# Router stage of a three-part transformer kernel: normed rows from TensorE transposes and ScalarE copies instead of GpSimd, slot table from bf16 products

## What is computed

```
x = layer_norm(ALPHA * x + h, ln_g[0], ln_b[0])          # 512 x 1024
g_logits = xf @ w_rg + b_rg                              # 512 x 4
g_idx = argmax(g_logits)
e_logits = (xf @ w_re + b_re).reshape(T, 4, 8)           # 512 x 32
top_v, top_i = top_k(e_logits of the group g_idx, 2)
order = argsort(flat_e)                                  # tokens' slots, sorted by expert
xbuf[slot_dest] = repeat(xf, 2)                          # rows gathered by expert
...                                                      # experts' three matmuls on xbuf
x = layer_norm(ALPHA * x + f, ln_g[1], ln_b[1])
```

## Time and profile before

| | us |
|---|---|
| median of 3 runs | 2987.75 |
| lowest, highest | 2985.99, 2991.82 |
| time of the profiled execution | 2988.24 |
| its span, first to last instruction | 2986.4 |
| PE busy in the span | 2835.5 (95%) |
| DVE, ACT, POOL busy | 2187.5 (73%), 1498.5 (50%), 497.3 (17%) |
| mean granted clock of TensorE, as a share of the full one | 0.975 |
| the router, from the mixer's last product (227.1) to the experts' first (284.3) | 57.2 |

### The profile page before, as it was taken

The page is one execution under the profiler, slowest core; times in us unless marked ns, Lnnn a source line. Parts: engine busy times, 40 slices in busy tenths (PEclk is TensorE's granted clock), DMA queues, the critical chain, the costliest instruction groups (busy, mean ns, idle before and its releaser), DMA issues.

```text
span 2986.4 us, 41805 instructions
## 1 busy us (share of the span) xinstructions
PE 2835.5 (95%) x16000; PEld 2449.8 (82%) x16000; DVE 2187.5 (73%) x2917; ACT 1498.5 (50%) x1995; POOL 497.3 (17%) x504
## 2 busy tenths in 40 slices
PE   8995999999958999999999999899999999999997
PEld 6674788888847999888888999799998888889996
DVE  6637899999978777666458776887776665687775
ACT  6823788888845444433335444454443332354443
POOL 3214011111012111110113111121111111121111
PEclk9997999999978999999999999999999999999998
DMA  5152999999945555232335646365543332355551
GB/s 215 50 174 90 349 376 373 374 374 380 375 167 140 158 162 157 94 108 88 98 99 135 180 132 177 105 163 148 171 137 99 100 99 94 99 148 156 160 159 57
DMA packets 170155, 516.25 MB, mean 173 GB/s; under 512 B 21600, under 2 KB 22112, under 8 KB 169696
## 3 DMA queue, kind: packets, MB, share of 16 engines
q1 hardware_dynamic: 130176, 422.38, 39.9%
q0 software_dynamic: 37568, 79.72, 12.6%
q10 hardware_dynamic: 2208, 11.43, 1.0%
HBM read 509.24 MB, written 12.58 MB: 175 GB/s over the span
## 4 chain that ended last, share of the span: by engine, by line
PE 81%; DVE 7%; issue 4%; ACT 3%; DMA 2%; POOL 2%; SPq 0%; DVEq 0%; ACTq 0%; POOLq 0%
PE bank L597 27%; PE bank L595 27%; PE bank L596 27%; DVE w_lo L1658 1%; ACT w_hi L1035 1%; PE bank L601 1%; DMA sums<-in_w_b 1%; DVE ft L2033 0%; DMA raw<-in_rec_in 0%; DMA raw<-in_w_b 0%; DVE xT L2084 0%; DMA raw<-in_w_a 0%; POOL mv L1461 0%; DVE st L1748 0%; DVE rsq L2069 0%
## 5 line engine op out<-in xcount | busy, mean ns | idle before, releaser
L1658 DVE TENSOR_TENSOR w_lo<-raw,w_hi 128x1024 fp32r<-128x1024 f32 (+3 forms) x481 | 593.1, 1250 | 286.6 <-ACT w_hi L1035 279.5
L1035 ACT ACTIVATE w_hi<-raw 128x1024 fp32r<-128x1024 f32 (+1 forms) x491 | 507.7, 1046 | 291.1 <-PE bank L597 284.1
L595 PE MATMUL bank<-xf_hi,w_lo 128*128 128x256 f32 x2112 | 593.2, 281 | 48.5 <-DVE xf_lo L2039 22.0
L597 PE MATMUL bank<-xf_hi,w_hi 128*128 128x256 f32 x2112 | 589.8, 279 | 0.0
L596 PE MATMUL bank<-xf_lo,w_hi 128*128 128x256 f32 x2112 | 589.8, 279 | 0.0
L595 PEld LDWEIGHTS bank<-xf_hi,w_lo 128*128 128x128 f32 x2112 | 401.8, 190 | 54.3 <-issue 23.7
L596 PEld LDWEIGHTS bank<-xf_lo,w_hi 128*128 128x128 f32 x2112 | 402.1, 190 | 2.4 <-issue 1.0
L597 PEld LDWEIGHTS bank<-xf_hi,w_hi 128*128 128x128 f32 x2112 | 401.9, 190 | 0.0
L1658 DVE TENSOR_TENSOR w_lo<-raw_more,w_hi 128x1024 fp32r<-128x1024 f32 x249 | 296.6, 1221 | 50.9 <-ACT w_hi L1035 48.2
L597 PE MATMUL bank<-g_hi,w_hi 128*128 128x512 f32 x832 | 327.5, 394 | 0.0
L596 PE MATMUL bank<-g_lo,w_hi 128*128 128x512 f32 x832 | 325.7, 392 | 0.0
(11 more groups left out here) (336 smaller groups left out, 5206.9 us busy)
## 6 DMA issues: line engine op xcount, KB each, us to landing
raw_more<-in_moe SPq DMA_DIRECT2D x249, 512.0 KB, 6.5
raw<-in_moe SPq DMA_DIRECT2D x135, 512.0 KB, 6.6
raw<-in_w_a SPq DMA_DIRECT2D x77, 512.0 KB, 6.4
raw<-in_w_b SPq DMA_DIRECT2D x76, 512.0 KB, 6.1
raw<-in_w_in SPq DMA_DIRECT2D x73, 512.0 KB, 3.6
sums<-in_w_a POOLq DMA_DIRECT2D x88, 256.0 KB, 4.9
sums<-in_w_b POOLq DMA_DIRECT2D x88, 256.0 KB, 4.9
raw<-in_w_a SPq DMA_DIRECT2D x68, 256.0 KB, 6.1
```

The costliest lines, as they stand in the source:

```text
L595: e.matmul(out, a_lo, b_hi, start=start, stop=False, skip_group_check=partial)
L597: return e.matmul(out, a_hi, b_hi, start=False, stop=stop, skip_group_check=partial)
L1035: e.activation(split_of(k)[0], source_of(k), ACT.Copy).then_inc(s["hi"], 1)
L1658: e.tensor_tensor(lo, source_of(k), hi.bitcast(F32), ALU.subtract).then_inc(s["lo"], 1)
```

## The change

It has three parts.

1. POOL's four pairs of multiply and add, its four writes of rows and the two loads of `gb` go. In their place PE turns the finished `x1T` back, 32 transposes (`back`, 8 banks), behind the transposes of the logits and ahead of the ranks. ACT copies the 8 banks into `x_tok` (128 x 512 each) behind its last copies into `x1T`, and after each second one waits for its own copies and issues the write of that tile. All of that stands ahead of ACT's two exponentials of the gates. POOL's clearing of `xe` now waits for the last of the transposes back.
2. The last four of the 32 copies into `x1T` (tile 3, upper half) go from ACT to DVE, and the last logits wait for the two halves apart.
3. The slots' numbers are split in a multiple of 32 and a rest, so that each is exact in bf16. `oneh` and the two products `numb` are bf16, and the table is 16 bf16 products instead of 8 float32 ones. DVE makes one small product more.

The diff, cut to its core:

```
 bank_table:
-            use(("turn", tt, half), "x1t", 8 * tt + 4 * half + 4)
+            use(("turn", tt, half), *(("x1t", 8 * tt + 4 * half + 4) if (tt, half) != (TT - 1, 1) else ("x1v", 1)))
     use("lgt", "lgc", 2)
+    for tt in range(TT):
+        for half in range(2):
+            use(("back", tt, half), "x1g", 2 * tt + half + 1)

 tensor_program, logits:
+                if tt < TT - 1:
                     e.wait_ge(s["x1t"], 8 * tt + 8)
                 for k in range(DT):
+                    if tt == TT - 1 and k % 4 == 0:
+                        e.wait_ge(*((s["x1v"], 1) if k else (s["x1t"], 8 * tt + 4)))
...
+            for tt in range(TT):
+                for half in range(2):
+                    b = free_bank(("back", tt, half))
+                    transpose4(lambda n: x1T[:, 4 * half + n, tt * P:(tt + 1) * P], b).then_inc(s["turn"], 1)
...
             for n in range(2 * TT):
-                f = e.matmul(b[:, 0:NBLK], oneh[:, n, :], blkh[:, n, :], start=n == 0, stop=n == 2 * TT - 1)
+                e.matmul(b[:, 0:NBLK], oneh[:, n, :], numb[:, 0, n, :], start=n == 0, stop=False)
+                f = e.matmul(b[:, 0:NBLK], oneh[:, n, :], numb[:, 1, n, :], start=False, stop=n == 2 * TT - 1)

 scalar_program:
-            e.dma_start(gb[:, 0, :], io["ln"][0:1, :].partition_broadcast(P)).then_inc(s["router"], 16)
-            e.dma_start(gb[:, 1, :], io["ln"][1:2, :].partition_broadcast(P)).then_inc(s["router"], 16)
...
+            for tt in range(TT):
+                for half in range(2):
+                    e.wait_ge(s["turn"], 2 * TT + 2 * tt + half + 1)
+                    e.activation(x_tok[:, tt, half * T:(half + 1) * T], bank_of(("back", tt, half))[:, :], ACT.Copy) \
+                        .then_inc(s["x1g"], 1)
+                e.wait_ge(s["x1g"], 2 * tt + 2)
+                e.dma_start(x1_dram[tt * P:(tt + 1) * P, :], x_tok[:, tt, :]).then_inc(s["x1d"], 16)

 pool_program:
-            for tt in range(TT):
-                x = x_tok[:, tt, :]
-                e.wait_ge(s["turn"], 2 * tt + 2)
...
-                e.tensor_tensor(x, x, gb[:, 0, :], ALU.mult).then_inc(s["x1g"], 1)
-                e.wait_ge(s["x1g"], 2 * tt + 1)
-                e.tensor_tensor(x, x, gb[:, 1, :], ALU.add).then_inc(s["x1g"], 1)
-                e.wait_ge(s["x1g"], 2 * tt + 2)
-                e.dma_start(x1_dram[tt * P:(tt + 1) * P, :], x).then_inc(s["x1d"], 16)
...
-            e.wait_ge(s["lgm"], TT)
+            e.wait_ge(s["turn"], 4 * TT)
             e.memset(xe[:, :, :], 0.0).then_inc(s["rows"], 1)

 vector_program:
+            e.wait_ge(s["turn"], 2 * TT)
+            for n in range(4):
+                f = e.tensor_scalar(x1T[:, 4 + n, (TT - 1) * P:], bank_of(("turn", TT - 1, 1))[:, n * P:(n + 1) * P],
+                                    par("ln_g", 4 + n), par("ln_b", 4 + n), ALU.mult, ALU.add)
+            f.then_inc(s["x1v"], 1)
...
             e.tensor_tensor(
-                blkh[:, :, :], blkh[:, :, :],
-                consts[:, C_SLOT:C_SLOT + 2 * TT].unsqueeze(2).to_broadcast([P, 2 * TT, NBLK]), ALU.mult).then_inc(s["idx"], 1)
+                numb[:, 0, :, :], blkh[:, :, :],
+                consts[:, C_SLOT:C_SLOT + 2 * TT].unsqueeze(2).to_broadcast([P, 2 * TT, NBLK]), ALU.mult)
+            e.tensor_tensor(
+                numb[:, 1, :, :], blkh[:, :, :],
+                consts[:, C_REST:C_REST + 2 * TT].unsqueeze(2).to_broadcast([P, 2 * TT, NBLK]), ALU.mult).then_inc(s["idx"], 1)
```

More of the change, by code:

```diff
@@ L72 @@
 C_SLOT = C_EROW + TT * NE
-C_ROW4 = C_SLOT + 2 * TT
+C_REST = C_SLOT + 2 * TT
+C_ROW4 = C_REST + 2 * TT
 C_EDGE = C_ROW4 + 1
@@ L306 @@
 smm snap spa spp spr sq sqr srec stm stt sum tbm th tmc tmf tmm tsm turn un used uu vv wsum wt x1d x1g x1t xgf
-xgh xgl xhi xhi2 xin xlo xlo0 xn xn2 xnv xr xtn yea yev yhi ylo yy zf zp zz""".split()
+x1v xgh xgl xhi xhi2 xin xlo xlo0 xn xn2 xnv xr xtn yea yev yhi ylo yy zf zp zz""".split()
 def build(nc, io):
@@ L349, in build @@
                 raw_more = sb("raw_more", [P, NMORE, W], into=moe)
-                gb = sb("gb", [P, 2, D], into=moe)
                 st = sb("st", [P, TT, 20], into=moe)
@@ L361, in build @@
                 place = sb("place", [P, 8, 2 * TT], into=moe)
-                oneh = sb("oneh", [P, 2 * TT, P], into=moe)
+                oneh = sb("oneh", [P, 2 * TT, P], BF16, moe)
                 blkh = sb("blkh", [P, 2 * TT, NBLK], into=moe)
+                numb = sb("numb", [P, 2, 2 * TT, NBLK], BF16, moe)
                 tabs = sb("tabs", [P, 4, NBLK], into=moe)
@@ L645, in logits @@
             def logits(tt):
-                e.wait_ge(s["x1t"], 8 * tt + 8)
+                if tt < TT - 1:
+                    e.wait_ge(s["x1t"], 8 * tt + 8)
                 for k in range(DT):
+                    if tt == TT - 1 and k % 4 == 0:
+                        e.wait_ge(*((s["x1v"], 1) if k else (s["x1t"], 8 * tt + 4)))
                     f = e.matmul(bank[7][0:NG + NE, tt * P:(tt + 1) * P], wr[:, k, :], x1T[:, k, tt * P:(tt + 1) * P],
@@ L652, in tensor_program @@
             e.wait_ge(s["par"], 32)
-            e.wait_ge(s["router"], 64)
+            e.wait_ge(s["router"], 32)
             for tt in range(TT):
@@ L1122, in scalar_program @@
                     a = tt - 1
-                    for half in range(2):
+                    for half in range(2 if a < TT - 1 else 1):
                         e.wait_ge(s["turn"], 2 * a + half + 1)
@@ L1477, in pool_program @@
                 weights(2 * RT + k)
-            for tt in range(TT):
-                x = x_tok[:, tt, :]
-                e.wait_ge(s["turn"], 2 * tt + 2)
-                if tt == 0:
-                    e.wait_ge(s["router"], 64)
-                e.tensor_tensor(x, x, gb[:, 0, :], ALU.mult).then_inc(s["x1g"], 1)
-                e.wait_ge(s["x1g"], 2 * tt + 1)
-                e.tensor_tensor(x, x, gb[:, 1, :], ALU.add).then_inc(s["x1g"], 1)
-                e.wait_ge(s["x1g"], 2 * tt + 2)
-                e.dma_start(x1_dram[tt * P:(tt + 1) * P, :], x).then_inc(s["x1d"], 16)
             def gather(n):
@@ L2420, in lay_out @@
     a["params"] = np.concatenate([columns(groups[n]) for n, _ in PARAM_GROUPS], axis=1)
-    a["ln"] = np.stack([f["ln_g"][0, 0], f["ln_b"][0, 0]])
     a["wr"] = np.concatenate([f["moe_w_group"][0], f["moe_w_expert"][0]], axis=1) \
@@ L2458, in lay_out @@
         for tt in range(TT):
-            c[:, C_SLOT + k * TT + tt] = k * T + tt * P + np.arange(P) + 1
+            number = k * T + tt * P + np.arange(P) + 1
+            c[:, C_SLOT + k * TT + tt] = number - number % 32
+            c[:, C_REST + k * TT + tt] = number % 32
     c[:, C_ROW4] = 4 * np.arange(P)
```

## The result

The changed kernel takes 3031.3 us (median of 4 runs, 3027.4 to 3034.6), the kernel before 2986.9 (4 runs, 2985.0 to 2991.8). The ratio is 1.0144, with a 95% interval of 1.0128 to 1.016: it is 44 us slower, where 8 us faster was forecast.

A forecast was written before the change was run, and what follows sets the result against it. PE was busy nearly everywhere, but the router was one chain of short work. Terms 3.15 + 2.51 + 2.97 - 0.42 = 8.21 us took 2988.24 to 2980.0, as a median 2979.5 us; range 2975.0 to 2985.5.

The forecast's parts named there:

- Each of these costs nothing: Router gap behind the logits: added PE, ACT and POOL work, `gb` loads and moved bank ring cost 0 us.
- C: Rival at the experts' start: the gain is given back there; if half, 2983.6 us; chance 0.07.
- the ring: PSUM banks: moved on one place; experts' first banks wait for ACT's copies back, done long before; no cost.
- The sum of 8.21 for the router: Router: three terms less one extra DVE product, 3.15 + 2.51 + 2.97 - 0.42 us gained.
- First term: Router's first part: without POOL's work norms take 0.81 us and logits come earlier, gaining 3.15 us (2.3 to 3.8).
- second: Two DVE steps behind the logits, lines 1804 and 1807, fall to 0.17 us each, gaining 2.51 us.
- Third term: Table of slots: bf16 products cut 3.63 us to 0.66, gaining 2.97; one more DVE product costs 0.42.
- The added work in the gap: Behind the logits: PE's 4.1 us with 1.8 cover, ACT's 7.4 us, writes with 9 us cover; no cost.
- Rival A: Router: transposes back run at half clock and the ranks wait for them; gain 7.2 us, 2980.5 us; chance 0.15.
- the clock: Router: the transposes back were taken at full clock, following logits without a pause above a us; 4.1 us.
- Rival B: Router: POOL did not hold DVE's norms and steps; only 2.55 us gained, 2985.2 us; chance 0.05.
- rival D: Experts: full clock comes later because the table shrinks; with 34 us more at half clock, 2994 us; chance 0.03.

The follow-up runs named there:

- before_pad32: The kernel before with 32 unused bytes per partition ahead of `ones`, nothing else changed: 3025.2 us, ratio 1.0133.
- onecol: The changed kernel with the slots' rests in one column of constants instead of eight, so later feed-forward and mixer tensors keep their old addresses: 2984.9 us, 0.9988.
- onecol_ring: onecol with the ring of PSUM banks moved on by six more places behind the transposes `fin`, no unused bytes: 2980.4 us, 0.9970.
- ring_back: onecol with 128 unused bytes ahead of `sil`, 64 ahead of `e_hi`, and the bank ring moved on six places right behind the table: 2960.0 us, 0.9907.
- rows_only: onecol with `oneh` and `blkh` in float32 and the table's eight float32 products as before: router's stage 47.99 us, one run.
- table_only: The kernel before with the bf16 table alone and one column of rests, rows by GpSimd as before: router's stage 51.03 us, one run.
- pool_noise: onecol with GpSimd multiplying an unused tensor, twice per tile once it is transposed, nothing waiting for it: router's stage 48.94 us, one run.
- before_all32: The kernel before with 32 unused bytes ahead of the first large tensor, so raw and split weights move with the activations: 2987.5 us, 1.0004.
- after_e64: The changed kernel with unused bytes: 96 ahead of `ones`, 64 ahead of `sil` and 64 ahead of `e_hi`: 2993.4 us, 1.0027.

## Why the prediction was wrong

**The total was wrong by 52 us, and the failed step is the sentence "Each of these costs nothing" on what the change adds and moves.** It went through PE's, ACT's and POOL's work, the loads and the ring. It did not look at where the tensors lie. Eight more columns of constants stood in the diff, and neither the sum nor any rival asked what moves with them. They moved `xf`, `g` and `xg` by 32 bytes against `w`, and some 10,900 products lost 3 to 6 ns each on average. before_pad32 and onecol show this from both sides: the loss comes without the change, and the change without the loss. No rival contained it; C, which had a gain lost behind the router, put it into the experts, which were 2 us faster.

**In the same sentence the ring was wrong.** "The ring of banks is moved on by one place; the experts' first banks now wait for ACT's copies back, which are done long before." That checked the first user behind the change. The wait came 2,000 us later, 4.5 us at the start of layer 2's mixers, and a gain of 2.3 us came ahead of the first feed-forward part. onecol_ring against onecol, 4 us, shows the first; ring_back, where the gain is gone, the second.

**The sum of 8.21 for the router nearly held.** With the addresses of before and the wait gone, onecol_ring is 8.6 us faster than its runs of before (0.9970, 0.9959 to 0.9981; forecast 0.9972), and its 2980.4 lies in the forecast's range. That the total agrees so well is in part luck. Other stages of its profile differ from before too: the experts by -3.4 us, the stretch behind them by -2.1, the first feed-forward part by +2.3, the two next by +3.5. So I rather go by the router's stage, 53.32 to 45.59: 7.7 us, 0.5 less than the sum. By its terms:

- *First term, 3.15, and second, 2.51:* together 5.66; rows_only measured 5.3. DVE read the logits at 246.76, forecast 246.8, but the whole trace ran 0.6 ahead there, so the first term was 0.6 short: logits 0 took 3.28 where I had kept 2.73, with a granted clock of 0.58 in 235.90 to 239.20 against 0.70 in 237.00 to 239.80 before. That PE and not DVE would be late next was right: DVE's third norm ended at 237.8 and PE came to it at 239.12. DVE's four copies took 1.37, forecast 1.3.
- *Third term, 2.97 less 0.42:* the table took 0.63, forecast 0.66. The second small product cost 0.34, since it starts before the first has ended. table_only gained 2.3, forecast 2.55.
- *The added work in the gap:* right. PE had 2.3 us of cover left, ACT's writes were issued by 254.6 and landed in 2.6 us each, the first gather waited for `gidx` alone.
- *Rival A and the clock:* the transposes back ran at the full clock, as the first of two windows of the changed kernel shows (us, busy time of PE, PEld, DVE, ACT and POOL with what overlaps the window, granted clock, DMA share, GB/s), and faster than the 4.1 us that I took (3.71):

```profile
248.00:252.00 4.00, 3.63 (x32) 3.40 (x32) 3.49 (x15) 2.54 (x5) 0.30 (x1) 1.00 0.33 131
...
280.00:284.00 4.00, 4.00 (x19) 3.22 (x18) 3.16 (x3) 2.90 (x4) 0.00 (x0) 1.00 0.66 215
```

By the rule of the Trainium skill ("TensorE: Matmul & The Clock Gate", section "Part 4: PE-mode transpose") that transposes don't count as work for the clock, case A would have come. It did not; but they stood right behind logits and lasted under 4 us, so this trace does not refute the rule either.
- *Rival B* is out by the norms of 0.81 and by pool_noise, *rival D* by the second window: the experts' products began at 276.0, and 4 us on they had the full clock, where before they began at 284.3 and had 0.52 of it in 286 to 290. D had called the table the one stretch of PE's work in the 20 us ahead of the experts; there were also eight transposes, at 280.84 before and 272.56 now.

## What to carry to other kernels

A diff that changes the size of a tensor moves all that is allocated behind it: compare the addresses of the operands of the bulk of the work, and read the distance from one product's start to the next in a window that holds the same products, since the page's mean length only hints at it. Keep such a tensor's size inside its padding or put it last, and search the distance on purpose: here 192 unused bytes were worth 17 us. Where buffers are handed out in a ring, an inserted use moves every user behind it, so look at the ends of all stages and not only at the next user.

## What the runs showed of the hardware

I had not expected that the pitch of PE's products depends on where the two operands lie in SBUF relative to each other. It went by the distance modulo 512 bytes in the kernels run here, in steps as fine as 32 bytes; by the mean of a group in the feed-forward parts and the experts, products of 256 columns were 113 to 120 ns apart, products of 512 columns 227 to 235, at the full clock and with PE busy without a gap. The absolute address did not matter (before_all32), and the experts' stage agrees to within 3 us across kernels with the same distance. `raw` kept its distance to `w` in all runs, so what is called the distance to `w` is one to `raw` as well; but PE does not read `raw`, and in after_e64 the products with `e` changed when only `e` had moved. What ran just before can count too, as those of `xf` behind `e` show. Which distances are good differs between the two widths and between the roles of the operands. Why, no run here shows. I did not try distances below 32 bytes, and of the 16 steps in 512 bytes four were seen in the feed-forward parts and seven in the experts, so there may be better ones.
